# Hybrid attention, pooling and MoE block on one core: the first expert's first two rows of weight tiles go into dead activation buffers, and their slot goes to the third expert

## The reference

```
h2 = rms_norm(x, norm2_g)
logits = h2 @ router_w + router_b                 # 32 experts
gates = softmax(top_4(logits))
per expert e, on its tokens:
    gu  = h2 @ w_gate_up[e] + b_gate_up[e]        # 1024 x 2048
    gate = min(gu[:, :1024], 7);  up = clip(gu[:, 1024:], -7, 7)
    out = (gate * sigmoid(1.702 * gate) * (up + 1)) @ w_down[e] + b_down[e]   # 1024 x 1024
x = x + sum over chosen experts of gate * out
```

## Time and profile before

| | |
|---|---|
| median of 3 runs | 1105.47 us (1105.36 to 1105.55) |
| profiled execution, its own time | 1106.94 us |
| its span in the trace | 1105.0 us |
| PE busy | 1059.7 us, 96% |
| DVE, ACT, POOL busy | 326.6, 118.1, 8.2 us |
| granted TensorE clock, mean of the span | 0.998 |
| DMA | 430.33 MB, mean 389 GB/s |

### The profile page before, as it was taken

The page is one execution under the profiler, slowest core; times in us unless marked ns, Lnnn a source line. Parts: engine busy times, 40 slices in busy tenths (PEclk is TensorE's granted clock), DMA queues, the critical chain, the costliest instruction groups (busy, mean ns, idle before and its releaser), DMA issues.

```text
span 1105.0 us, 12147 instructions
## 1 busy us (share of the span) xinstructions
PE 1059.7 (96%) x4838; PEld 429.9 (39%) x4838; DVE 326.6 (30%) x649; ACT 118.1 (11%) x210; POOL 8.2 (1%) x17
## 2 busy tenths in 40 slices
PE   9999999999999999999999989898989899999988
PEld 6445446443434343434433324242424243333322
DVE  2554123222232322222222222222222222222321
ACT  3124102100000000000000000000000000000001
POOL 2000000000000000000000000000000000000000
PEclk9999999999999999999999999999999999999999
DMA  9952484899999999999999999999999999999996
GB/s 331 391 188 103 173 370 157 329 424 413 429 427 429 427 429 428 431 428 428 429 427 429 429 429 428 428 428 428 429 427 429 429 429 427 429 428 428 428 428 274
DMA packets 40562, 430.33 MB, mean 389 GB/s; under 512 B 4049, under 2 KB 6225, under 8 KB 15713
## 3 DMA queue, kind: packets, MB, share of 16 engines
q1 hardware_dynamic: 39568, 428.11, 92.5%
q0 software_dynamic: 688, 1.91, 0.5%
q10 hardware_dynamic: 288, 0.08, 0.0%
HBM read 429.03 MB, written 1.05 MB: 389 GB/s over the span
## 4 chain that ended last, share of the span: by engine, by line
PE 64%; DMA 33%; SPq 1%; issue 1%; DVE 0%; ACT 0%; DVEq 0%
DMA slot<-w_gate_up_dram 33%; PE bank L1236 21%; PE bank L1263 14%; PE bank L939 9%; PE bank L1180 5%; PE bank L963 4%; PE bank L1252 2%; PE bank L1197 2%; PE bank L1158 1%; SPq L270 1%; PE bank L912 1%; PE bank L1290 1%; DMA slot<-w_in_dram 1%; PE bank L1221 0%; PE bank L1278 0%
## 5 line engine op out<-in xcount | busy, mean ns | idle before, releaser
L1236 PE MATMUL bank<-slot,scr 128*64 128x512 f32 x2048 | 469.9, 598 | 24.9 <-DMA slot<-w_gate_up_dram 24.9
L1236 PEld LDWEIGHTS bank<-slot,scr 128*64 128x64 f32 x2048 | 136.2, 136 | 323.2 <-issue 258.3
L1263 PE MATMUL bank<-slot,scr 128*64 128x512 f32 x992 | 225.4, 596 | 11.2 <-DMA slot<-w_down_dram 10.5
L854 DVE TENSOR_TENSOR x<-bank,x 128x512 f32<-128x512 f32 x120 | 77.3, 686 | 233.4 <-PE bank L1197 233.4
L1263 PEld LDWEIGHTS bank<-slot,scr 128*64 128x64 f32 x992 | 67.6, 137 | 142.3 <-issue 118.5
L829 DVE COPY scr<-bank 128x512 f32<-128x512 f32 x32 | 22.1, 692 | 288.1 <-PE bank L1236 288.1
L939 PE MATMUL bank<-slot,scr 128*128 128x512 f32 (+1 forms) x256 | 102.5, 549 | 0.7 <-DMA slot<-w_in_dram 0.7
L835 DVE TENSOR_TENSOR scr<-bank,bgu 128x512 f32<-128x512 f32 x64 | 41.2, 686 | 106.0 <-PE bank L1252 106.0
L1197 PE MATMUL bank<-scr 64*128 64x512 f32 x240 | 67.8, 641 | 0.0
L939 PEld LDWEIGHTS bank<-slot,scr 128*128 128x128 f32 x256 | 47.0, 190 | 42.0 <-issue 37.3
L1180 PEld LDWEIGHTS bank<-scr,xn 128*128 128x128 f32 x480 | 57.7, 196 | 12.2 <-issue 12.2
(11 more groups left out here) (187 smaller groups left out, 394.8 us busy)
## 6 DMA issues: line engine op xcount, KB each, us to landing
slot<-w_gate_up_dram SPq DMA_DIRECT2D x127, 2048.0 KB, 29.4
slot<-w_down_dram SPq DMA_DIRECT2D x63, 2048.0 KB, 22.8
slot<-w_in_dram SPq DMA_DIRECT2D x12, 1024.0 KB, 14.6
slot<-w_out_dram SPq DMA_DIRECT2D x4, 1024.0 KB, 4.9
slot<-w_in_dram SPq DMA_DIRECT2D x4, 580.0 KB, 8.6
slot<-w_branch_pool_dram SPq DMA_DIRECT2D x2, 1024.0 KB, 14.0
slot<-w_branch_attn_dram SPq DMA_DIRECT2D x2, 1024.0 KB, 11.3
slot<-w_gate_up_dram SPq DMA_DIRECT2D x2, 1024.0 KB, 6.4
```

What stands on the lines that cost most here:

```text
L854: V.tensor_tensor(x[:, b, 512 * h:512 * h + 512], XY[h][:, :], x[:, b, 512 * h:512 * h + 512], ALU.add).then_inc(read[f"Y{j}"], 1)
L1236: ins = MM(GB[h][T * g:T * g + T, :], xgT[:, k, T * e:T * e + T], gu_slot[s][:, c0:c0 + 512], start=k == 0, stop=k == KC - 1)
L1263: ins = MM(DB[T * h:T * h + T, :], actT[e][:, c, :], v3(dn_slot[j][:, :], 4)[:, k, 512 * h:512 * h + 512], start=c == 0, stop=c == KC - 1)
```

## The change

Two rows of expert 0's first slot no longer go to `gu_slot[0]`. Its row k=0 (1 MiB) is loaded into `scr[:, 2048:4096]` once the merged result has been transposed (`TJ_M + 4`), and its row k=1 into `scr[:, 0:2048]` once the router's last matmuls are done (`TJ_R[1] + 1`), which on SP's queue stands behind the two loads of `w_down`. `gu_slot[0]` is loaded with expert 2's first slot right behind that, with no wait on the gate_up of expert 0. The two half loads of expert 2 are now those of `gu_slot[1]`, after steps k=2 and k=3. The router's tables move to parts of `scr` in the old `sigp`, the down biases are loaded after step k=0 of expert 0, behind the router's weights. No arithmetic changes.

```diff
@@ buffers @@
-        rr = actT_t
+        early = [scr[:, 2048:4096], scr[:, 0:2048]]
+        ra, rb = scr[:, 5376:5632], scr[:, 5888:6144]
+        lgp, rwork, rex = v3(ra[:, 0:80], NB), v3(ra[:, 80:160], NB), v3(ra[:, 160:224], NB)
+        msk, gex, notm = v3(rb[:, 0:64], NB), v3(rb[:, 64:128], NB), v3(rb[:, 128:192], NB)
+        first_cnt, first_off = ra[:, 224:256], rb[:, 192:224]
...
+        early_in, early_used = [sem(f"early_in{k}") for k in range(2)], sem("early_used")
@@ SP @@
-            for s in range(2):
-                halves_used(s)
-                load_gu(s, 0)
+            sp.sem_inc(gu_in[0], 16)
+            halves_used(1)
+            load_gu(1, 0)
             sp.wait_ge(t_ready, TJ_O + 2)
             load_gu(2, 0)
...
             load_gu(7, 1)
+            sp.wait_ge(t_ready, TJ_M + 4)
+            sp.dma_start(early[0], gu_src(0, 0)[:, 0:HW]).then_inc(early_in[0], 16)
             for j in range(DN_SLOTS):
                 halves_used(4 + j)
                 load_dn(j, 0)
...
+            sp.wait_ge(t_ready, TJ_R[1] + 1)
+            sp.dma_start(early[1], gu_src(0, 0)[:, HW:UW]).then_inc(early_in[1], 16)
+            halves_used(0)
+            load_gu(0, 2)
             sp.wait_ge(first_used, 1)
-            sp.dma_start(gu_slot[0][:, 0:HW], gu_src(2, 0)[:, 0:HW]).then_inc(first_in, 16)
-            sp.wait_ge(gu_used[0], 1)
-            sp.dma_start(gu_slot[0][:, HW:UW], gu_src(2, 0)[:, HW:UW]).then_inc(gu_in[0], 16)
-            gates_a(2, 1, 1, 4)
+            sp.dma_start(gu_slot[1][:, 0:HW], gu_src(2, 1)[:, 0:HW]).then_inc(first_in, 16)
+            sp.wait_ge(gu_used[1], 1)
+            sp.dma_start(gu_slot[1][:, HW:UW], gu_src(2, 1)[:, HW:UW]).then_inc(gu_in[1], 16)
+            gates_a(2, 1, 2, 4)
@@ POOL @@
-            pool_e.wait_ge(t_ready, TJ_M + 4)
+            pool_e.wait_ge(merged_ready, NB)
+            pool_e.dma_start(rw, router_d.rearrange("(k p) e -> p k e", p=P)).then_inc(rw_in, 16)
+
+            pool_e.wait_ge(early_used, 1)
             for h in range(2):
                 pool_e.dma_start(bd_sb[E * h:E * h + E, :], b_dn[:, 512 * h:512 * h + 512]).then_inc(bd_in, 16)
-
-            pool_e.wait_ge(merged_ready, NB)
-            pool_e.dma_start(rw, router_d.rearrange("(k p) e -> p k e", p=P)).then_inc(rw_in, 16)
@@ PE, gate_up @@
-                    if k % 2 == 0:
-                        pe.wait_ge(gu_in[s], landed)
+                    if first and k < 2:
+                        pe.wait_ge(early_in[k], 16)
+                        w = early[k]
+                    else:
+                        if k % 2 == 0:
+                            pe.wait_ge(gu_in[s], landed)
+                        w = gu_slot[s][:, HW * (k % 2):HW * (k % 2) + HW]
...
-                    if k == 0 and whole_first:
-                        ins.then_inc(first_used, 1)
+                    if first and k in (0, 2):
+                        ins.then_inc((early_used, None, first_used)[k], 1)
```

More of the change, by code:

```diff
@@ L476, in _ @@
                 act.wait_ge(lg_ready, b + 1)
-                nc.scalar.activation(rr[:, 128 + 32 * b:160 + 32 * b], rr[:, 40 * b:40 * b + E], ACT.Exp,
+                nc.scalar.activation(rex[:, b, :], lgp[:, b, 0:E], ACT.Exp,
                                      bias=small[:, 190 + b:191 + b]).then_inc(ex_ready, 1)
@@ L715, in _ @@
                 tcopy(TJ_M + 2 * b + 1, hT[:, 4:8, b * P:b * P + P])
[L717 to L723, removed]
             tops = small[:, 204:220]
@@ L1101, in _ @@
             short_read(pe, TJ_M + 2)
-            msk = v3(rr[:, 640:704], NB)
             def router(b, halves):
@@ L1222, in gates_by_slot, with gate_up @@
                 ins.then_inc(done["S"], 1)
-            def gate_up(e, landed, copied, taken, between, whole_first=False):
+            def gate_up(e, landed, copied, taken, between, first=False):
                 for h in range(2):
@@ L1230, in gate_up @@
                         pe.wait_ge(read[f"X{k // 4}"], taken)
-                    if k % 2 == 0:
-                        pe.wait_ge(gu_in[s], landed)
+                    if first and k < 2:
[5 more added lines that the diff above has]
+                        w = gu_slot[s][:, HW * (k % 2):HW * (k % 2) + HW]
                     for h in range(2):
                         for g in range(2):
-                            c0 = HW * (k % 2) + D * g + 512 * h
+                            c0 = D * g + 512 * h
                             ins = MM(GB[h][T * g:T * g + T, :], xgT[:, k, T * e:T * e + T],
-                                     gu_slot[s][:, c0:c0 + 512], start=k == 0, stop=k == KC - 1)
+                                     w[:, c0:c0 + 512], start=k == 0, stop=k == KC - 1)
                     if k % 2 == 1:
                         ins.then_inc(gu_used[s], 1)
-                    if k == 0 and whole_first:
-                        ins.then_inc(first_used, 1)
+                    if first and k in (0, 2):
+                        ins.then_inc((early_used, None, first_used)[k], 1)
                     for at, call in between:
@@ L1321, in _ @@
             gather_rest()
-            gate_up(0, 16, 1, 1, [(3, gates_turned), (5, turn_biases)], whole_first=True)
+            gate_up(0, 16, 1, 1, [(3, gates_turned), (5, turn_biases)], first=True)
             short_read(pe, TJ_RANK[1] + 1)
```

## The result

| | before | changed |
|---|---|---|
| median of 20 runs each | 1105.26 us (1103.98 to 1107.21) | 1106.93 us (1106.07 to 1109.10) |
| ratio | | 1.0016, 95% interval 1.0010 to 1.0022 |
| profiled execution and its span | 1106.94, 1105.0 us | 1106.07, 1104.3 us |

The change costs 1.7 us, which is just within 0.2%, where the prediction had 1.9 us gained: the forecast was wrong in sign, and the time lies above its range. Note that the two profiled executions stand the other way round than the medians. The one of before was 1.7 us above its median, the one of the change the fastest of its 20 runs. Compared with each other they hide the loss. In the profile of before the clock had fallen shortly ahead of expert 0, and that turns out to be the first half of the explanation.

A forecast was written before the change was run, and what follows sets the result against it. The prediction took the stream of weight loads to bound the kernel. -2.0 us for the filled hole and +0.1 for the stall gave -1.9, so 1103.6 us against the median of 1105.47; 8 in 10 range 1102.6 to 1105.7.

The forecast's parts named there:

- What bounds the end: End of the kernel: it hangs on when the last gate_up weights land; PE goes at the loads' pace from 560 us.
- the signs that the prediction named: Profile after the change: last gate_up load lands at about 1073.2, PE's DMA waits some 33.5 us in place of 35.4.
- A PE stall before 560 us costs nothing by itself: Before 560 us: a PE stall costs only if it delays a slot's release while the queue is dry.
- The term s = 0.1 us, the dead heat,: Expert 0, step k=1: second early half lands at 197.25, step due at 197.2; stall 0.1 us, bounds none and 2.2.
- The term of 2.0 us for the hole: Weight stream: filling the some 4.6 us hole at 193.7 to 197.4 puts it 2.0 us ahead from 270 us on.
- The first early half: Load issued at 162.2 us, read by PE at 195.4: costs nothing, slack of over 20 us covers it.
- the biases: Down biases moved from 162.2 to about 197.5 us, read first at 243.75: cost nothing, without that cover 0.3 us.
- limit of 358 GB/s: Second early half: at this rate it needs 2.93 us instead of 2.45, making s 0.6 and the sum -1.4 us.
- B: Expert 0, step k=1: half lands late, a 2.2 us stall takes the gain back, 1105.7 us; chance 0.12, shared with another rival.
- C: Expert 0, step k=1: stall plus four microseconds at half clock, s = 4.1, so 1107.6 us; chance 0.08.
- A: Down load at 262.1 us: slowest DMA engine escapes the dry-queue start, gain towards 2.9 us, time 1102.9; chance 0.25.

The follow-up runs named there:

- the long one: Changed kernel with the second early half issued behind slot 0's load for expert 2 instead of ahead of it; 1113.39 us, ratio 1.0079 against the kernel before.
- the one-row version: Changed kernel with row k=1 loaded to slot 0 as before and only slot 0's first half loaded for expert 2 at once; 1105.41 us, ratio 1.0001 against before.
- the one with only the early halves: Changed kernel with slot 0 loaded for expert 2 in two halves after k=0 and k=1, as before; 1106.44 us, ratio 1.0014 against the kernel before.
- the version without the stall: Changed kernel with the second early half issued ahead of the second down load; 1104.62 us, ratio 0.9997 against before; run again 1104.27 us, ratio 0.9991.

## Why the prediction was wrong

**What bounds the end** was right: the last gate_up load, at the pace of the stream, and PE's waits from 560 us on. The extra work at the end costs 0.2 us, and the nearly constant 773.2 to 773.9 us above says the same, with one exception. Of the signs that the prediction named, the last gate_up load landed at 1074.3 and not at 1073.2, and PE's waits for DMA from 560 us on add up to 35.5 us (24.5 and 11.0) and not to 33.5.

**"A PE stall before 560 us costs nothing by itself"** was wrong in size and is the sentence that misled. The text took back half of it in the next clause, where the queue is dry, but the sum gave each later load 2.0 to 2.9 us to spare. 1.75 us of work ahead of k=1 cost 1.6 us. The reason stands in the prediction's own limits: with loads that land 7.7 us after issue at best and were landing at 9.7, the stream follows PE's releases, so a lead is cut down and a delay is handed on. The next point but one shows how little of those 9.7 us was room.

**The term s = 0.1 us, the dead heat,** is the step that failed. The landing was right (197.25 predicted, 196.3 to 197.3 measured), in part by luck: the half is issued at 188.6 to 188.8 instead of 189.5 and takes 7.7 to 8.5 us instead of 7.75. The other side, "step k=1 is due at 197.2", came from a profile in which the clock had halved during the gather; the fall of the clock stood in the text, but only as a rival's threat, not as a thing that had already moved PE's start. At full clock k=1 is due at 193.5 + 1.8 = 195.3. The stall was 1.1 to 2.0 us in the four profiles that have it (1.12, 1.79, 1.89, 1.97), beside the 7.0 us of the long one. That the profiled execution was 1.5 us above the median was said too, and put "in no term"; 1.5 us is also what the gather lost to the clock, but the second profile of that kernel, at full clock, is 1.0 us above the same kernel's median in its turn, so that the two are the same 1.5 us is not shown. The load moved ahead by one place removes 2.3 us.

**The term of 2.0 us for the hole** was mis-sized. About 1 us shows without the stall (1104.2 against 1105.2 at full clock), nothing in the one-row version, nothing between the changed kernel and the one with only the early halves. The 2.0 us were the difference of two landing times, 9.7 and 7.7 us, taken as time in which the load waits in the queue. The parts say otherwise. The load on the empty queue has its first part after 6.8 us and the last 0.9 us behind it; the one at 262.1 has them after 7.1 and 2.6 us behind. So 0.3 us was queue and 1.6 was spread, and filling the hole leaves the spread: in the changed kernel the same load has 7.1 and 2.4. What sets the spread is open; it varies by up to 2 us from profile to profile, and I have no run that holds it fixed. The hole's 4.6 us, which did not set the 2.0, is no difference of the prediction's rows either: from 193.7 to 197.4 it is 3.7, and the bytes that its windows lack from 193 to 199 are 5.0 us of the stream.

**The smaller terms.** The first early half cost nothing that shows (the one-row version, which has it, 1.0001), and neither did the biases at the end (1.0002 alone, and no difference without them). The Trainium skill's limit of 358 GB/s in "DMA: Bandwidth & Descriptors", section Specifications, was left aside rightly: 451 and 426 GB/s in the windows above. A sum by it (-1.4 us) would have been nearer to the result, but for a reason that the trace contradicts.

**The rivals.** B describes what happens, with a stall of 1.1 to 2.0 us where it had 2.2, and C what happens in one of the two profiles of the changed kernel. Both took 2.0 us off for the hole, so B's own time, 1105.7, is still 1.2 us short of the result. The chance of the two together, 0.20, was far too low. A did not happen in the changed kernel.

In sum, for the median run at full clock: about -1.0, if the gain of the version without the stall is taken as it stands, and +1.3 to +2.1 for the later start of k=1 (PE's start of k=1 after that of k=0 is 3.06 us in the first profile of the change and 3.91 in the second, against 1.8). This gives +0.3 to +1.1 of the 1.7 us. The remaining 0.6 us or more is of the size by which the gain may be missing whenever PE stalls, which the comparison with only the early halves suggests and does not prove. That the stall is what makes the change a loss is shown; the size of the loss is not fully accounted for.

## What to carry to other kernels

When two events come close to each other, take both times from a second profile, or from stretches at the clock that most runs have; a profile that is a microsecond slower than the median has its microsecond somewhere, and it may sit on the very number you need. Before a load is moved later, ask who waits for it at full speed, and put it ahead of loads that are needed long after: exchanging two loads on one queue turned a loss of 1.7 us into what is likely a gain of about 1. Filling a hole in a stream pays only as far as the loads behind it are not waiting for the consumer anyway. And a time to landing that is above the best one is not all queue: look at when the first part of the load lands before you count the difference as a lead.

## What was unexpected of the hardware

The granted clock answered to short idle stretches in an irregular way. In the second profile of the kernel before PE was busy for 0.63 and 0.79 of two windows and the clock stayed; in the first for 0.72 and 0.55, and it fell to 0.5:

```profile
190.00:191.00 1.00, 0.63 (x4) 0.52 (x4) 0.62 (x5) 0.99 (x3) 0.00 (x0) 1.00 0.88 377
191.00:192.00 1.00, 0.79 (x6) 0.79 (x7) 0.86 (x6) 0.15 (x1) 0.00 (x0) 1.00 0.95 410
```

The changed kernel had 0.72 and 0.54 in two windows in a row in its first profile, almost the numbers of the fall, and its clock stayed as well. It idled 1.12 us with no fall in that profile, and 1.97 us with one in the other; stalls of 1.79 and 1.89 us had none. Runs whose mean clock is below 0.9985 are 1.3 to 1.7 us longer in the medians above. And one 2 MiB load in the middle of a saturated stream took 9.9 and 11.5 us to land in two profiles of the same kernel. In the second the last of its 16 parts fell from 2.1 us behind the first, at the loads ahead of it, to 3.6, and it stayed that far behind to the end (3.7), a scatter as large as the effect under study.
